# Attention order on ScalarE and TensorE, and the depthwise convolution's taps on GpSimd, in a hybrid decoder step with expert retrieval

## The chip, the cores and the metric

The kernel runs on one core of one Trainium2 chip. The metric is the device time of one execution in microseconds. The core's engines are TensorE (PE), VectorE (DVE), ScalarE (ACT), GpSimd (POOL) and SyncE (SP); each runs its own list of instructions in order, and they wait for each other by semaphores. Sixteen DMA engines move data between HBM and the on-chip memory (SBUF).

## The reference

One layer of a decoder trunk, on 1024 prompt tokens and on 64 sample tokens (8 sequences of 8), all in float32. Per token of width 1024:

```
z = x @ w_in                        # q, k, v (8 heads x 64), GLU value a and gate g (512 channels)
att  = causal attention over a mixture of three dilations, merged by softmax denominators
glu  = a * sigmoid(g)
conv[t, ch] = sum_{k=0..30} w[k, ch] * glu[t - 30 + k, ch] + b[ch]     # depthwise, causal
conv = silu(LayerNorm(conv))
x1   = LayerNorm(ALPHA * x + concat(att, conv) @ w_out)
y    = LayerNorm(ALPHA * x1 + PEER(x1))
```

PEER picks 128 of 16384 experts for each token (8 heads, two sets of 128 keys, the best 16 of each, the best 16 of their sums). An expert is a row u and a row v of 1024 numbers. Its part of the output is `gate * gelu(x1 . u) * v`.

## The kernel before

**Tiles and stages.** The tokens are cut into 8 prompt tiles of 128 tokens (`PT = 8`) and one tile of 64 sample tokens. The program runs in stages n = -1 to 9. Stage n does two things side by side: the expert sums of tile n, and the *front* of tile m = n + 1, that is attention, convolution, output projection, the first LayerNorm and the routing that picks the experts. Each stage has 128 places q = 4 g + i, with g = 0 to 31 and i = 0 to 3, and every engine's list is written out by the same loops over g and i. So the order of the work on each engine is fixed by hand, by the place in which a function is called.

**Expert sums of tile n.** For slot s (place q = s in stages 1 to 7) GpSimd issues a gather (L618): an indirect DMA that brings one expert row of 8 KB to each of the 128 partitions, 1 MB in all, into a ring of 9 rows (4 rows for tile 0). GpSimd waits for the ring row: the pair of slots that used it must have been summed by TensorE (semaphore `pv`; for tile 0 `v_done` of VectorE). Up to here its list holds nothing but the 1088 gathers. VectorE takes the dot product of x1 with u (`dot`, L1053, place s). For each two slots ScalarE applies Gelu (L770, in the same place), VectorE multiplies by the gate and spreads the weights on a diagonal (`weigh`, L1061 and L1064, one place later), and TensorE adds the two rows v, weighted, in PSUM (`values_pair`, L1399 and L1403, one place later). Tile 0 sums on VectorE instead (`first_values`, L1079).

**The front of tile m.** Attention has one head per group g, as a pipeline over four engines. Before the change, head h passes through these places:

- TensorE `scores` (L1270) in group h, i = 3: q times k into PSUM bank 2 and 3. It waits for the maximum of head h-1 (`sm_done`) and for the scaled copy of head h-2 (`att_done`).
- VectorE `weights_max` (L952, L955) in group h+1, i = 2: adds the bias and takes the maximum.
- ScalarE `weights_exp` (L685) in group h+1, i = 2: Exp with the sum.
- TensorE `weights_T` (L1281) and ScalarE `weights_T` (L694) in group h+1, i = 3: transposes and their copy to `pT`.
- TensorE `values` (L1292) in group h+2, i = 1: weights times v, into PSUM bank 2. As the scores of head h+1 lie in the same bank, it waits for their maximum, which VectorE takes in group h+2, i = 2.
- VectorE `weights_sum` (L962) in group h+2, i = 1, and ScalarE `normalise` (L702) in group h+2, i = 1: the copy of the result to `att`, scaled by one over the sum. It waits for the values matmuls (`pv_done`).

ScalarE loads a table when it goes from Gelu to Exp and back.

**Convolution.** The GLU output of all tokens is in HBM (`glu_scratch`). For tile m SyncE issues the load of its 158 columns into `gl` (L524) once the routing of tile m-1 is done (`a_route`). VectorE then runs 31 taps, `taps(m, k)`, spread over the places q = 1 to 39 by `tap_at`. Each tap is four instructions of 128x128, one for each 128 channels (L917 for k = 0, L920 for the rest). In group 10, i = 1, TensorE transposes the sums (`conv_rows`, L1309) when the semaphore `cv` shows them complete, and LayerNorm, Silu and the output projection follow. Tile 0's taps (L941, L944) and those of the sample tile (L929, L932) have their own lines.

**The rest of a stage.** In places 6 to 11 VectorE ends the tile before (`residual`, `ln2_end`). From place 69 to 127 VectorE runs the routing of tile m (L998 to L1030), one head in 7 places.

Of the kernel before, what the change touches and what calls it, by code (L numbers as in the profile page):

```python
# [10 lines left out]
ALU = mybir.AluOpType  # L11
# [3 lines left out]
P = 128  # L15
# [6 lines left out]
PT = SEQ // P  # L22
TILES = PT + 1
# [3 lines left out]
CT = CC // P  # L27
CK = 31
# [8 lines left out]
PH = 8  # L37
# [138 lines left out]
def tap_at(q):  # L176
    return range(q * CK // TAP_SPAN, (q + 1) * CK // TAP_SPAN) if q < TAP_SPAN else range(0)
# [31 lines left out]
def build(nc, I, O):  # L209
# [5 lines left out]
    with ctx:  # L215
# [3 lines left out]
        def at(off, shape, dt=F32):  # L219
            names[0] += 1  # L220
            return nc.alloc_sbuf_tensor_at(f"t{names[0]}", shape, dt, offset=base + off)

        def sem(name):
            return ctx.enter_context(nc.semaphore(name))
# [14 lines left out]
        qT = at(o_s, [P, CT, P])  # L239
        conv = at(o_s + 2048, [P, CT, P])  # L240
        cn = at(o_s + 4096, [P, CC])
        sm = at(o_s + 6144, [P, 2, SEQ])
        pT = at(o_s + 16384, [P, SEQ])
        att = at(o_s + 20480, [P, AW])
# [100 lines left out]
        pads = sem("pads")  # L345
        glu_done = sem("glu_done")
        cv = sem("cv")
        cvs = sem("cvs")
        q_out = [sem(f"q_out{i}") for i in range(2)]
        glu_out = [sem(f"glu_out{i}") for i in range(3)]  # L350
# [84 lines left out]
        def slots(t):  # L435
            return SLOTS if t < PT else SLOTS // 2
# [159 lines left out]
        @block.gpsimd  # L596
        def _(pool):
            def gather(t, s):
                if s % TOP == 0 and t < PT:
                    pool.wait_ge(a_route, PH * t + s // TOP + 1)  # L600
                elif s == 0:
                    pool.wait_ge(id_up, 16)
                r, use = spot(t, s)
                if t == 0:
                    if s >= FIRST_RING:
                        pool.wait_ge(v_done, s - FIRST_RING + 1)
                else:
                    k = (t - 1) * SLOTS + s
                    if k >= RING:
                        pool.wait_ge(pv, (k - RING) // 2 + 1)  # L610
                    elif k < FIRST_RING:
                        pool.wait_ge(v_done, SLOTS - FIRST_RING + k + 1)
                    elif k == FIRST_RING:
                        pool.wait_ge(proj_done, len(UNITS))
                        pool.wait_ge(glu_done, 3 * CT)
                        for i in range(2):
                            pool.wait_ge(q_out[i], 64)
                pool.indirect_dma_start(ring[:, r, :], None, I["expert_uv"],  # L618
                                        bass.IndirectOffsetOnAxis(ap=idn[t % 2][:, s:s + 1], axis=0)).then_inc(landed[r], 16)

            for t in range(TILES):
                for s in range(slots(t)):
                    gather(t, s)

        @block.scalar
        def _(act):
# [201 lines left out]
                                x1_rows(PT)  # L828

            def front(m, g, i):  # L830
                if i == 1 and 2 <= g < PH + 2:
                    normalise(m, g - 2)
                if i == 2 and 1 <= g <= PH:
                    weights_exp(m, g - 1)
                if i == 3 and 1 <= g <= PH:
                    weights_T(m, g - 1)
                for h in range(PH):
                    if g == QUERY_AT[h] and i == 3:
                        query_copy(m, h)
                        if h == 0:  # L840
                            x1_rows(m)
                if i != 2:
                    return
                if g == 11:
                    conv_std(m)
                if g == 12:
                    conv_swish(m)
                    attended(m)
                    route_loads(m)
                if g == 14:  # L850
                    ln1_std(m)
                if g == 15:
                    x1_transposed(m)
                for h in range(PH):
                    if g == QUERY_AT[h] + 1:
                        score_copy(m, h)
# [31 lines left out]
        def _(dve):  # L888
# [19 lines left out]
                    dve.wait_ge(state_in, 16)  # L908
                    dve.tensor_copy(gluS[:, i, :, PAST:], glu_st[:, i % 3, tn:tn + sn].rearrange("p (b t) -> p b t", b=NB)).then_inc(glus_kept, 1)

            def taps(m, k):
                if k == 0:
                    dve.wait_ge(gl_in, 16 * m)
                for i in range(CT):
                    w, src, dst = cwT[:, i, k:k + 1], gl[:, i, k:k + P], conv[:, i, :]
                    if k == 0:
                        dve.tensor_scalar(dst, src, w, cwT[:, i, CK:CK + 1], ALU.mult, ALU.add).then_inc(cv, 1)  # L917
                    else:
                        dve.wait_ge(cv, TAPS * m + CT * (k - 1) + i + 1)
                        dve.scalar_tensor_tensor(dst, src, w, dst, ALU.mult, ALU.add).then_inc(cv, 1)  # L920

            def sample_taps(k):
                if k == 0:
                    dve.wait_ge(glus_kept, CT)
# [10 lines left out]
            for i in range(CT):  # L935
                gated(0, i)
                dve.wait_ge(glu_done, i + 1)
                for k in range(CK):
                    w, src, dst = cwT[:, i, k:k + 1], gl[:, i, k:k + P], conv[:, i, :]
                    if k == 0:  # L940
                        dve.tensor_scalar(dst, src, w, cwT[:, i, CK:CK + 1], ALU.mult, ALU.add).then_inc(cv, 1)  # L941
                    else:
                        dve.wait_ge(cv, CK * i + k)
                        dve.scalar_tensor_tensor(dst, src, w, dst, ALU.mult, ALU.add).then_inc(cv, 1)  # L944

            def weights_max(m, h):
                u = PH * m + h
# [217 lines left out]
                    gates_end(PT, gate_events(PT), range(PH))  # L1165

            def front(m, g, i):
                for k in tap_at(4 * g + i) if m else ():
                    taps(m, k)
                if i == 1 and 2 <= g < PH + 2:  # L1170
                    weights_sum(m, g - 2)
                if i == 2 and 1 <= g < PH + 1:
                    weights_max(m, g - 1)
                if g == 11 and i == 0:
                    conv_var(m)
                if g == 11 and i == 3:
                    conv_norm(m)
                if g == 14 and i in (0, 1):
                    ln1_half(m, i)
                if g == 15 and i == 0:  # L1180
                    ln1_end(m)
                h, at_ = divmod(4 * g + i - ROUTE_AT, ROUTE_STEP)
                if 0 <= h < PH:
                    if at_ in (0, 2):
                        route_side(m, h, at_ // 2)
                    if at_ == 4:
                        route_pairs(m, h)
                    if at_ == 5:
                        route_experts(m, h)
                if m == 0 and at_ == ROUTE_STEP - 1 and 0 <= h < EARLY_GATES:  # L1190
                    gates(0, range(h, h + 1))
                if m == 0 and at_ == 1 and 1 <= h <= EARLY_GATES:
                    gates_end(0, h, range(h - 1, h))
                if g == 31 and i == 1:
                    gates(m, range(0 if m else EARLY_GATES, PH))
                if g == 31 and i == 3:
                    gates_end(m, gate_events(m), range(0 if m else EARLY_GATES, PH))
# [35 lines left out]
        def _(pe):  # L1233
# [66 lines left out]

            def conv_rows(m):
                if m < PT:
                    pe.wait_ge(cv, TAPS * (m + 1))
                    pe.wait_ge(sm_done, PH * (m + 1))
                else:
                    pe.wait_ge(cvs, TAPS)
                src = conv if m < PT else convS
                for c in range(CT):
                    last = pe.transpose(bank[3][0:rows(m), c * P:(c + 1) * P], src[:, c, :], ident[:, :])  # L1309
                last.then_inc(c_tr, 1)  # L1310
# [171 lines left out]
                                x1_rows(PT)  # L1482

            def front(m, g, i):
                if i == 1 and 2 <= g < PH + 2:
                    values(m, g - 2)
                if i == 3 and 1 <= g < PH + 1:
                    weights_T(m, g - 1)
                if i == 3 and g < PH:
                    scores(m, g)  # L1490
                for h in range(PH):
                    if g == QUERY_AT[h] and i == 3:
                        queries(m, h)
                        if h == 0:
                            x1_rows(m)
                    if g == QUERY_AT[h] + 1 and i == 1:
                        key_scores(m, h)
                if g == 13 and i in (1, 3):
                    out_projection(m, i // 2)
                if i != 1:  # L1500
                    return
                if g == 10:
                    att_transposes(m)
                    conv_rows(m)
                if g == 12:
                    conv_back(m)
                if g == 15:
                    x1_transposes(m)
# [68 lines left out]
```

## Time and profile before

| | us |
|---|---|
| median of 3 runs | 3743.29 |
| lowest, highest | 3739.91, 3750.01 |
| the profiled execution | 3747.08 |
| its span, first to last instruction | 3745.3 |

| engine | busy us | share of the span |
|---|---|---|
| VectorE | 2799.2 | 75% |
| TensorE, matmuls | 2592.0 | 69% |
| GpSimd | 1236.1 | 33% |
| ScalarE | 681.2 | 18% |

How to read it: the durations come from one profiled execution, whose own time is the 3747.08 us, and its instructions fill 3745.3 us of it. The queue of the gathers moved 1140.92 MB and its packets took 76.1% of the time of the 16 DMA engines; all queues together moved 1385.68 MB, a mean of 370 GB/s. The mean granted TensorE clock was 0.826 of full speed.
### The profile page before, as it was taken

The numbers are of one execution on the slowest core, as the hardware profiler recorded it, in microseconds if no ns is written. First come the engines' busy times: TensorE is split into PE (matmuls) and PEld (weight loads), VectorE is DVE, ScalarE is ACT, GpSimd is POOL, SyncE is SP. The second block draws the span as 40 slices with busy tenths as digits, with TensorE's granted clock in tenths as the row PEclk, the third lists the DMA queues.
The fourth block names the chain that finished last, engine by engine and source line by source line (L and its number), as shares of the span: only waits on it lengthen the run. The fifth ranks groups of instructions, "written<-read, shape, count | busy, mean of one in ns | idle before, by whom it ended". The sixth has DMA issues, their size and how long they took to land.

```text
span 3745.3 us, 39494 instructions
## 1 busy us (share of the span) xinstructions
PE 2592.0 (69%) x13744; PEld 1193.5 (32%) x13744; DVE 2799.2 (75%) x7472; ACT 681.2 (18%) x1478; POOL 1236.1 (33%) x1092
## 2 busy tenths in 40 slices
PE   7864347736775777677677766776787666779766
PEld 5433124532232223233323332333233322234311
DVE  5177867898789868986897689768976894356965
ACT  1210122002200321032013200320132002121000
POOL 0022212123443444434443434344434432233242
PEclk8987668867887888888788888887888878889889
DMA  9977898979999999999999999999989999999698
GB/s 341 343 296 258 303 371 311 400 278 355 398 417 381 361 381 421 395 367 375 415 391 347 381 421 390 344 369 421 393 336 368 420 409 422 418 420 396 261 384 342
DMA packets 217512, 1385.68 MB, mean 370 GB/s; under 512 B 27417, under 2 KB 38169, under 8 KB 66649
## 3 DMA queue, kind: packets, MB, share of 16 engines
q0 software_dynamic: 156672, 1140.92, 76.1%
q1 hardware_dynamic: 40384, 142.88, 10.4%
q10 hardware_dynamic: 20256, 99.35, 6.7%
q8 instruction: 109, 1.79, 0.2%
q14 instruction: 91, 0.74, 0.1%
HBM read 1369.94 MB, written 80.04 MB: 387 GB/s over the span
## 4 chain that ended last, share of the span: by engine, by line
DVE 30%; PE 26%; DMA 25%; issue 13%; ACT 3%; POOL 2%; ACTq 0%; SPq 0%; DVEq 0%; POOLq 0%
DMA t<-in_expert_uv,t 25%; PE psum L1403 12%; DVE t L1053 8%; PE psum L1250 3%; PE psum L1292 3%; DVE psum L1079 2%; PE psum L1328 2%; POOL t L618 2%; PE psum L1360 2%; DVE t L1064 2%; DVE t L1001 2%; DVE t L999 2%; PE psum L1270 2%; DVE t L1002 2%; DVE t L1000 1%
## 5 line engine op out<-in xcount | busy, mean ns | idle before, releaser
L618 POOL DMA_INDIRECT t<-in_expert_uv,t x1088 | 1235.9, 1136 | 2479.9 <-PE psum L1399 982.0
L1403 PE MATMUL psum<-t,t 64*64 64x512 f32 x4576 | 1323.4, 717 | 652.0 <-DVE t L1064 651.4
L1053 DVE CUSTOM_DVE_ANT_0 t<-t,t 128x1024 f32<-128x1024 f32 x1088 | 1322.2, 1222 | 529.6 <-DMA t<-in_expert_uv,t 520.0
L1399 PE MATMUL psum<-t,t 64*64 64x512 f32 x2592 | 807.9, 753 | 0.0
L1403 PEld LDWEIGHTS psum<-t,t 64*64 64x64 f32 x4576 | 329.0, 154 | 1422.6 <-DVE t L1064 798.4
L770 ACT ACTIVATE t<-t 128x2 f32<-128x2 f32 x544 | 110.6, 203 | 2038.0 <-DVE t L1053 2037.0
L1360 PEld LDWEIGHTS psum<-t,t 128*128 128x128 f32 x2304 | 286.3, 206 | 72.2 <-issue 63.4
L1360 PE MATMUL psum<-t,t 128*128 128x128 f32 (+1 forms) x2304 | 296.6, 291 | 4.8 <-ACT t L740 4.8
L1250 PE MATMUL psum<-t,t 128*128 128x128 f32 (+2 forms) x768 | 269.7, 512 | 6.6 <-DMA t<-in_xT 6.1
L920 DVE SCALAR_TENSOR_TENSOR t<-t,t,t 128x128 f32<-128x128 f32 x840 | 238.0, 346 | 0.0
L1292 PE MATMUL psum<-t,t 128*128 128x64 f32 x576 | 105.9, 348 | 162.7 <-issue 162.2
L1399 PEld LDWEIGHTS psum<-t,t 64*64 64x64 f32 x2592 | 182.3, 157 | 0.0
L1250 PEld LDWEIGHTS psum<-t,t 128*128 128x128 f32 x768 | 137.7, 210 | 123.3 <-issue 116.6
L1061 DVE TENSOR_TENSOR t<-t,t 128x2 f32<-128x2 f32 x480 | 75.9, 158 | 128.4 <-ACT t L770 126.3
L1079 DVE SCALAR_TENSOR_TENSOR psum<-t,t,psum 128x1024 f32<-128x1024 f32 x127 | 163.8, 1290 | 4.9 <-DVE t L1071 0.5
L1292 PEld LDWEIGHTS psum<-t,t 128*128 128x128 f32 x576 | 97.3, 256 | 211.1 <-issue 209.9
L1064 DVE TENSOR_TENSOR t<-t,t 128x128 f32<-128x128 f32 x480 | 140.2, 292 | 16.6
L1396 PE MATMUL psum<-t,t 128*64 128x512 f32 x256 | 118.9, 611 | 44.7 <-DVE t L1064 44.7
L1328 PE MATMUL psum<-t,t 128*128 128x512 f32 (+1 forms) x288 | 131.9, 614 | 3.6 <-ACT t L706 3.6
L770 ACT ACT_TABLE_LOAD x103 | 132.1, 1283 | 1.8
L1374 PE MATMUL psum<-t,t 128*128 128x128 f32 (+1 forms) x288 | 53.9, 316 | 112.4 <-ACT t L751 111.9
L1270 PE MATMUL psum<-t,t 64*128 64x512 f32 (+3 forms) x192 | 88.3, 571 | 39.7 <-DMA t<-q_scratch 39.2
(136 smaller groups left out, 2122.2 us busy)
## 6 DMA issues: line engine op xcount, KB each, us to landing
t<-in_wq_t ACTq DMA_DIRECT2D x63, 1024.0 KB, 9.6
out<-in_cache_k_win SPq DMA_DIRECT2D x8, 4080.0 KB, 46.2
out<-in_cache_v_win SPq DMA_DIRECT2D x8, 4080.0 KB, 40.9
t<-in_w_in_t ACTq DMA_DIRECT2D x44, 512.0 KB, 7.5
t<-in_kc_t SPq DMA_DIRECT2D x8, 2560.0 KB, 18.6
t<-in_vc_t SPq DMA_DIRECT2D x8, 2560.0 KB, 14.0
t<-in_expert_uv,t POOLq DMA_INDIRECT x1088, 11.0
t<-in_w_v_t ACTq DMA_DIRECT2D x6, 1024.0 KB, 10.0
```

The costliest lines, as they stand in the source:

```text
L618: pool.indirect_dma_start(ring[:, r, :], None, I["expert_uv"], bass.IndirectOffsetOnAxis(ap=idn[t % 2][:, s:s + 1], axis=0)).then_inc(land ...
L770: act.activation(d_, d_, ACT.Gelu).then_inc(a_gelu, 1)
L920: dve.scalar_tensor_tensor(dst, src, w, dst, ALU.mult, ALU.add).then_inc(cv, 1)
L1053: dve.tensor_tensor_reduce(out=ring[:, r, 0:D], in0=x1[t % 2][:, :], in1=ring[:, r, 0:D], scale=1.0, scalar=0.0, op0=ALU.mult, op1=ALU.add ...
L1064: dve.tensor_tensor(zt[:, k % Z_RING, :, :], ident2[:, :].unsqueeze(1).broadcast_to([P, 2, NS]), d2.unsqueeze(2).broadcast_to([P, 2, NS]), ...
L1079: dve.scalar_tensor_tensor(first_sum, ring[:, r, D:ROW], w_, first_sum, ALU.mult, ALU.add).then_inc(v_done, 1)
L1250: last = pe.matmul(dst[:, 0:tn + sn], w_ring[:, r, k, :], xT[p][:, k, 0:tn + sn], start=(k == 0), stop=(k == KD - 1))
L1292: last = pe.matmul(bank[2][:, 0:E], pT[:, j * P:(j + 1) * P], v[:, j, h * E:(h + 1) * E], start=(j == 0), stop=(j == m))
L1328: last = pe.matmul(bank[3 - half][0:rows(m), :], mixedT[:, k, 0:rows(m)], w_out[:, k, half * 512:(half + 1) * 512], start=(k == 0), stop=( ...
L1360: last = pe.matmul(bank[2 + h % 2][:, side * r:(side + 1) * r], w_[:, k, side * KEYC:(side + 1) * KEYC], x1T[:, k, 0:r], start=(k == 0), s ...
L1399: last = pe.matmul(AUX[t][half][NS - NS * a:P - NS * a, :], zt[NS * a:NS * a + NS, k % Z_RING, j, :], vv[NS * a:NS * a + NS, :], start=(c ...
L1403: last = pe.matmul(MAIN[t][half][NS * a:NS * a + NS, :], zt[NS * a:NS * a + NS, k % Z_RING, j, :], vv[NS * a:NS * a + NS, :], start=(c == ...
```

## The change

Three things change.

1. On ScalarE `normalise` of head g-2 moves from i = 1 of group g, ahead of `weights_exp` (i = 2), to i = 3 of the same group, behind `weights_exp` and the Gelu of that place and ahead of the copy of the transposed weights.
2. On TensorE `values` of head g-2 moves from i = 1 to i = 3 of group g, ahead of `weights_T` and `scores`.
3. The taps of tiles 1 to 7 leave VectorE. They run on GpSimd, in its list of gathers, in the same places (behind the gathers of the place). A tap is now a product of 128x512 with the weight spread along the tokens, into a new buffer `tap` (which lies where `cn` lies), and an addition of 128x512 to `conv`; each of the two waits for the one before. The first tap is the product straight into `conv` and the addition of the bias. The first tap of a tile waits for the load of `gl` and for the transposes of the tile before that read `conv`. The semaphore `cv` now counts GpSimd's instructions; tile 0's taps, which stay on VectorE, count on a new one, `cv0`.

```diff
@@ gpsimd
-            for t in range(TILES):
-                for s in range(slots(t)):
-                    gather(t, s)
+            def taps(m, k):
+                if k == 0:
+                    pool.wait_ge(gl_in, 16 * m)
+                    pool.wait_ge(c_tr, m)
+                n = 2 * CK * (m - 1) + 2 * k
+                w = cwT[:, :, k:k + 1].broadcast_to([P, CT, P])
+                if k == 0:
+                    pool.tensor_tensor(conv[:, :, :], gl[:, :, k:k + P], w, ALU.mult).then_inc(cv, 1)
+                    pool.wait_ge(cv, n + 1)
+                    w = cwT[:, :, CK:CK + 1].broadcast_to([P, CT, P])
+                    pool.tensor_tensor(conv[:, :, :], conv[:, :, :], w, ALU.add).then_inc(cv, 1)
+                else:
+                    pool.tensor_tensor(tap[:, :, :], gl[:, :, k:k + P], w, ALU.mult).then_inc(cv, 1)
+                    pool.wait_ge(cv, n + 1)
+                    pool.tensor_tensor(conv[:, :, :], conv[:, :, :], tap[:, :, :], ALU.add).then_inc(cv, 1)
+                pool.wait_ge(cv, n + 2)
+
+            for n in range(-1, TILES):
+                for q in range(SLOTS):
+                    for s in slots_at(n, q):
+                        gather(max(n, 0), s)
+                    for k in tap_at(q) if 1 <= n + 1 < PT else ():
+                        taps(n + 1, k)
@@ scalar, front(m, g, i)
-                if i == 1 and 2 <= g < PH + 2:
-                    normalise(m, g - 2)
                 if i == 2 and 1 <= g <= PH:
                     weights_exp(m, g - 1)
+                if i == 3 and 2 <= g < PH + 2:
+                    normalise(m, g - 2)
                 if i == 3 and 1 <= g <= PH:
                     weights_T(m, g - 1)
@@ vector, front(m, g, i)
-                for k in tap_at(4 * g + i) if m else ():
-                    taps(m, k)
@@ tensor, conv_rows(m) and front(m, g, i)
-                    pe.wait_ge(cv, TAPS * (m + 1))
+                    if m:
+                        pe.wait_ge(cv, 2 * CK * m)
+                    else:
+                        pe.wait_ge(cv0, TAPS)
...
-                if i == 1 and 2 <= g < PH + 2:
+                if i == 3 and 2 <= g < PH + 2:
                     values(m, g - 2)
```

## Rows read from the trace of the kernel before

**Rows 1.** The page, part 1: busy us, share of the span, instructions.
```profile
PE 2592.0 (69%) x13744; PEld 1193.5 (32%) x13744; DVE 2799.2 (75%) x7472; ACT 681.2 (18%) x1478; POOL 1236.1 (33%) x1092
```

**Rows 2.** Windows: places 0 to 40 of tiles 0 to 6, each engine's busy us.
```profile
core 0: us, PE busy (x) PEld busy (x) DVE busy (x) ACT busy (x) POOL busy (x), PEclk, DMA share, GB/s
434.90:574.90 140.00, 62.44 (x146) 32.08 (x144) 98.15 (x241) 37.80 (x67) 25.13 (x24) 0.62 0.93 349
847.90:974.20 126.30, 83.12 (x392) 29.78 (x392) 108.73 (x328) 37.74 (x70) 50.95 (x44) 0.77 0.90 356
1221.20:1346.00 124.80, 94.65 (x458) 35.51 (x454) 99.47 (x286) 40.06 (x72) 52.57 (x43) 0.85 0.89 348
1586.00:1712.90 126.90, 98.86 (x494) 41.84 (x490) 100.88 (x287) 41.71 (x72) 45.50 (x42) 0.84 0.89 348
1955.40:2089.40 134.00, 106.29 (x522) 47.28 (x518) 101.81 (x286) 43.57 (x72) 48.21 (x43) 0.83 0.87 329
2329.50:2465.40 135.90, 106.57 (x544) 47.42 (x540) 102.85 (x288) 44.94 (x72) 47.37 (x43) 0.86 0.86 325
2705.50:2844.00 138.50, 111.65 (x566) 50.20 (x562) 103.86 (x286) 46.75 (x72) 47.28 (x43) 0.86 0.84 322
```

**Rows 3.** Windows of tile 1: places 40 to 69, then 69 to 128.
```profile
974.20:1046.50 72.30, 56.57 (x328) 22.27 (x332) 51.53 (x130) 17.60 (x39) 33.22 (x29) 0.88 1.01 422
1046.50:1221.20 174.70, 111.84 (x708) 49.69 (x702) 165.28 (x508) 14.27 (x48) 65.48 (x56) 0.78 0.99 396
```

**Rows 4.** One attention head of tile 6: timeline (start, us, engine, line), then its window.
```profile
2783.24 1.97 PE L1292 MATMUL psum<-t,t 128*128 128x64 f32 x16 [2.86 <-issue]
2785.30 0.31 ACT L702 ACTIVATE t<-psum,t 128x64 f32<-128x64 f32 x1 [5.73 <-PE psum L1292]
2788.19 1.28 ACT L770 ACT_TABLE_LOAD   x1
2789.72 0.16 DVE L1061 TENSOR_TENSOR t<-t,t 128x2 f32<-128x2 f32 x1 [3.06 <-ACT t L770]
...
2783.24:2796.30 13.06, 10.29 (x60) 4.82 (x61) 9.89 (x29) 5.55 (x8) 4.45 (x5) 0.85 0.88 333
```

**Rows 5.** The page, part 5: the tap instructions, busy us and mean ns.
```profile
L920 DVE SCALAR_TENSOR_TENSOR t<-t,t,t 128x128 f32<-128x128 f32 x840 | 238.0, 346 | 0.0
```

**Rows 6.** Groups by line: elementwise instructions of VectorE, busy us and mean ns.
```profile
L1026 DVE TENSOR_TENSOR t<-t,t 128x512 f32<-128x512 f32 (+1 forms) x72 | 49.7, 691 | 2.5
...
L1108 DVE TENSOR_TENSOR t<-t,t 128x1024 f32<-128x1024 f32 (+1 forms) x9 | 11.0, 1224 | 0.3
```

**Rows 7.** Timeline: a dot, the gather that began under it, and the next.
```profile
2793.44 1.21 DVE L1053 CUSTOM_DVE_ANT_0 t<-t,t 128x1024 f32<-128x1024 f32 x1
2793.84 1.62 POOL L618 DMA_INDIRECT t<-in_expert_uv,t  x1 [2.82 <-PE psum L1399]
2795.77 0.94 POOL L618 DMA_INDIRECT t<-in_expert_uv,t  x1 [0.30 <-issue]
```

**Rows 8.** The line of the gathers: duration in ns, and landing.
```profile
L618 POOL DMA_INDIRECT t<-in_expert_uv,t x1088: 932/939/2182, 191.7 to 3715.3; - x182
...
DMA to landing us min/median/max: 5.4/11.0/38.3
```

**Rows 9.** Timeline and line: glu loads of tiles 1 and 6, landing, tile 6's start.
```profile
834.12 0.84 SPq L524 DMA_DIRECT2D t<-glu_scratch  x1
2699.56 0.63 SPq L524 DMA_DIRECT2D t<-glu_scratch  x1
...
DMA to landing us min/median/max: 5.3/8.7/9.3
...
2697.16 0.94 POOL L618 DMA_INDIRECT t<-in_expert_uv,t  x1 [0.30 <-issue]
2708.75 1.12 DVE L917 TENSOR_SCALAR t<-t,t 128x128 f32<-128x128 f32 x4 [0.47 <-DMA t<-glu_scratch]
```

More of the change, by code:

```diff
@@ L241, in build @@
         cn = at(o_s + 4096, [P, CC])
+        tap = at(o_s + 4096, [P, CT, P])
         sm = at(o_s + 6144, [P, 2, SEQ])
@@ L347, in build @@
         cv = sem("cv")
+        cv0 = sem("cv0")
         cvs = sem("cvs")
@@ L909, in gated @@
                     dve.tensor_copy(gluS[:, i, :, PAST:], glu_st[:, i % 3, tn:tn + sn].rearrange("p (b t) -> p b t", b=NB)).then_inc(glus_kept, 1)
[L911 to L920, printed above, removed]
             def sample_taps(k):
@@ L940, in _ @@
                     if k == 0:
-                        dve.tensor_scalar(dst, src, w, cwT[:, i, CK:CK + 1], ALU.mult, ALU.add).then_inc(cv, 1)
+                        dve.tensor_scalar(dst, src, w, cwT[:, i, CK:CK + 1], ALU.mult, ALU.add).then_inc(cv0, 1)
                     else:
-                        dve.wait_ge(cv, CK * i + k)
-                        dve.scalar_tensor_tensor(dst, src, w, dst, ALU.mult, ALU.add).then_inc(cv, 1)
+                        dve.wait_ge(cv0, CK * i + k)
+                        dve.scalar_tensor_tensor(dst, src, w, dst, ALU.mult, ALU.add).then_inc(cv0, 1)
             def weights_max(m, h):
```

## The prediction

> **What bounds the kernel now.** I read the page first: VectorE is busy 75% of the span, TensorE 69%, GpSimd 33% [rows 1]. No engine is full, so the bound changes from stage to stage and the page cannot say what one stage is worth. The second view cuts the span at the dot products, one for each of the 128 places of a tile. Tiles 1 to 6 (while the front of tiles 2 to 7 runs) take 365 to 376 us from first dot to first dot, in three parts. Places 0 to 40 take 124.8 to 138.5 us, 3.3 us a place, mean 131.1; VectorE is busy 75 to 86% of it, TensorE 66% (tile 1) to 81% (tile 6), the DMA engines 84 to 90% [rows 2]. Places 40 to 69 take 72.3 us, 2.5 a place, at 422 GB/s and a DMA share of 1.01: bound by the gathers' bytes. Places 69 to 128 have VectorE at 165.28 of 174.70 us, in the routing [rows 3]. Only the first part holds taps and attention. The third view is one head of attention in it, 13.06 us long for tile 6 (from the values matmuls of one head at 2783.24 to the next): TensorE had waited 2.86 us before those matmuls, since they need VectorE's maximum of the next head; ScalarE waited 5.73 us for them before its scaled copy, then came Exp, a table load and Gelu, and VectorE stood 3.06 us until that Gelu [rows 4]. So the part is a loop of VectorE, TensorE and ScalarE. GpSimd is busy only 46 to 53 us there [rows 2] and otherwise waits for free ring rows.
>
> **Taps off VectorE.** 840 instructions of 346 ns go, 120 per tile [rows 5], with 4 of L917: 34 us busy of the 102 in an average part, about 0.85 us a place. VectorE's own need falls to some 68 us in 131; it can't bound the part afterwards.
>
> **The scaled copy and the values matmuls two places later.** Exp no longer stands behind a copy that waits for matmuls that wait for VectorE. Per head that can remove up to the 3.06 us on VectorE and the 2.86 us on TensorE [rows 4]; they lie beside each other, so about 3 us a head, 8 heads, at most 25 us a tile, if nothing else is late. In place of it TensorE runs values, transposes and scores back to back, and the scores of a head now wait in the same place for a copy queued behind a Gelu; the table load before Gelu is 1.28 us [rows 4], beside the matmuls. I cost that at nothing: after it the VectorE maximum is three places away. What is late next is the question, and I say GpSimd.
>
> **Taps on GpSimd, its serial need.** From place 1 to 39 it has 31 taps of two instructions, 62 of 128x512, each waiting for the one before. The trace holds no arithmetic of that size on GpSimd. Lower end: VectorE's multiply of 128x512, 0.69 us; upper end: twice VectorE's 128x1024, 2.45 us. I take 1.22, the 128x1024 one once [rows 6], that is half of VectorE's rate, because it lies nearest to the one instruction of size that GpSimd has, the gather with 0.94 to 2.18 us [rows 8]. For the wait between two I take 0.1 us, ends 0 and the 0.30 between two gathers [rows 7]. So 62 x 1.32 = 81.8 us. A gather is 0.94 us and 0.30 to the next [rows 7, 8]: 1.24.
> The Trainium skill (GPSIMD Engine Reference, "Performance versus the Vector engine") gives 4497 ns for a two-input f32 operation of 2048 elements, twice VectorE's. A quarter is an estimate of 1.12 us; by it the 62 would cost 75.6 us instead of 81.8, 6 us less a tile. No row here shows it.
>
> **What the two engines take from each other.** A dot (1.21 us) started at 2793.44 and ended at 2794.65; a gather that began under it at 2793.84 took 1.62 us and ended 0.81 us after the dot, while the next, beside other VectorE work, took 0.94 [rows 7]. Gathers run from 0.93 to 2.18 us [rows 8]. So a dot already holds up GpSimd. The taps read SBUF all the time, 82 us of a part, and there are 40 dots of 1.22 us, 49 us, besides the weighings (0.16 + 0.29 us per pair). Bounds of GpSimd's loss: 0, and each dot with half a weighing in full, 1.22 + 0.23 = 1.45 us, 55 us for 38. I take 0.6 a dot, 23 us: GpSimd is in a tap about half of the time, a dot that arrives then waits for its end and costs the next tap about a dot; the other half costs a gather a few tenths. VectorE loses about as much and has the 34 us to pay it with.
> The Trainium skill (SBUF — State Buffer, "Who interferes with whom") says that a VectorE instruction with two SBUF inputs contends with a GpSimd instruction that reads SBUF, and the second fully blocks. The row agrees for a gather under a dot; what it does to an elementwise instruction no run here shows. With that rule in full the loss is nearer the 55 us, without it 0.
>
> **The new wait.** The first tap waits for the load of glu rows. That load is issued (L524) 13.8 us before the first dot of tile 1 and about 6 us before it in tiles 2 to 6, and lands a median 8.7 us later; VectorE stood 0.47 us for it in tile 6 [rows 9]. But GpSimd is ahead of VectorE by the ring: in tile 6 the gather of slot 2 was issued at 2697.16, the load landed at about 2708.3 [rows 9]. It and those after it now stand behind the wait, and behind them the dots. A gather lands a median of 11.0 us after its issue [rows 8], so VectorE stands for them early in the tile.
>
> **The sum per tile.** From the landing of glu to the dot of place 40, GpSimd needs 38 gathers, 47.1, plus 81.8, plus 23: 152 us; then 11 us until slot 40 has landed: 163. Now the same stretch is, in order of tiles 1 to 6 (part's end from [rows 2], issue plus 8.7 from [rows 9]; the issues of tiles 2 to 5, which aren't shown, are 6.7, 6.0, 5.9 and 5.9 us ahead of their first dot): 131, 123, 124, 131, 133 and 136, mean 129.7. The difference is 33 us, six times 199. The places after 40 give nothing back: they run at the DMA limit or at VectorE's. Tile 0 has only 25 gathers in its first 40 places and takes 140 us for them [rows 2]: GpSimd needs 31 + 82 + 10 = 123; VectorE's 34 us come free but its four-row ring makes each gather's latency count, and a gather now stands behind taps. I put it at 0, ends -20 and +20. The tail and the sample tile have no part in it.
> The profiled execution took 3747.1 us (span 3745.3); 3747.1 + 199 = 3946. The median of the runs is 3743.3, 3.8 lower: **3942 us**, 5.3% slower.
>
> **Rivals.**
> - GpSimd keeps up: faster. The two stretches are equal when 47.1 + 62x + lock = 118.7, so with 23 us lost to the dots a tap instruction with its wait must cost under 0.78 us, without any loss under 1.15. Then the part falls to the next bound: bytes at 422 GB/s, 126.3 x 356 / 422 = 107 us, and TensorE's 112 us in tile 6, in sum some 130 less over six tiles; the wait at the tile's start keeps about 40 of it, tile 0 gives 20: 3747 - 110, median 3633. For it: the loop of rows 4 does lose 3 us a head. Against: it needs GpSimd nearly at VectorE's rate. 20%.
> - GpSimd is serial, but the two don't block each other: 47.1 + 81.8 - 118.7 = 10 us, 62 in all: 3805. Against it stands the gather stretched by a dot. 12%.
> - Everything cancels within 0.3%: a tap instruction at the balance point. 3%.
> - A tap instruction costs 2 us or more, from the stride of the input or from changing between gathers and arithmetic: 47.1 + 62 x 2.1 + 30 = 207, 89 a tile, 532: 4275. 8%.
> The likeliest, GpSimd bound with blocking, has 57%, with its own range 3850 to 4050 (lost to the dots 12 to 35 us, a tap instruction with its wait 1.25 to 1.42: 18 to 51 us a tile).
>
> **Range and chances.** Uncertainty of the costs and the edge of the faster case: 3670 to 4090. It leaves out the dear instruction (8) and some 12 of the faster case. A measurement of this kernel tells 0.3%, 11 us, from no change. Faster 0.20, same 0.04, slower 0.76. The bounds taken all together (0.69 without loss, 2.45 with all) reach further, but no row favours either end.
>
> **What would show it.** Right: in places 0 to 40 GpSimd's busy share goes from 37% to over 80%, with almost no wait for TensorE between its gathers; VectorE's wait for landings there grows from a few us to tens, its busy time falls by less than 34 us because dots become longer than 1.22 us; DMA share falls below 0.8; places 40 to 128 are unchanged; the idle of L1061 behind ScalarE shrinks. The tap instruction's mean should be 1.1 to 1.6 us with the blocking. Wrong: GpSimd still waiting for TensorE in the part, a tap instruction under 0.8 us, dots of constant length, or a changed time after place 40.

## The result, and the profile after

The changed kernel takes 3944.2 us (median of 4 runs), the kernel before 3746.7 us beside it: ratio 1.0526, 95% interval 1.0503 to 1.0550. The forecast was 3942 us, 5.3% slower. (One of the four runs, at a granted TensorE clock of 0.544 in place of 0.82, took 4352.8 us; the interval is made without it.) The profiled execution spans 3939.4 us, 194.1 more than before.

The page after, parts 1, 2 and 5. The columns are as in [rows 1, 5]; L620 is now the gather, L1064 the dot, L635 the product and L637 the addition of a tap, L1072 and L1075 the weighing, L1415 the sums on TensorE.

```profile
span 3939.4 us, 39267 instructions
PE 2626.3 (67%) x13744; PEld 1184.7 (30%) x13744; DVE 2801.5 (71%) x6604; ACT 682.1 (17%) x1478; POOL 1880.8 (48%) x1526
POOL 0022562149634964396438744874478433223232
...
L620 POOL DMA_INDIRECT t<-in_expert_uv,t x1088 | 1265.1, 1163 | 1949.8 <-PE psum L1411 714.2
L1064 DVE CUSTOM_DVE_ANT_0 t<-t,t 128x1024 f32<-128x1024 f32 x1088 | 1451.6, 1340 | 873.9 <-DMA t<-in_expert_uv,t 864.0
...
L637 POOL TENSOR_TENSOR t<-t,t 128x512 f32<-128x512 f32 x210 | 365.3, 1739 | 16.5
...
L635 POOL TENSOR_TENSOR t<-t,t 128x512 f32<-128x512 f32 x210 | 231.4, 1102 | 4.8
...
L1072 DVE TENSOR_TENSOR t<-t,t 128x2 f32<-128x2 f32 x480 | 147.4, 307 | 13.0 <-ACT t L792 10.9
```

VectorE lost 868 instructions and is busy as long as before (2801.5 against 2799.2 us, [rows 1]). Its wait for gathers went from 520 to 864 us. GpSimd's line in 40 slices has a peak of 6 to 9 tenths at the start of each tile, where it had 4; in the chain of work that ended last, part 4 of the page, GpSimd has 19% of the span where it had 2%.

The windows of places 0 to 40 of tiles 1 to 6 answer to [rows 2]; columns as there. Then those of places 40 to 69 and 69 to 128 of tile 6.

```profile
856.40:1012.80 156.40, 87.50 (x392) 29.12 (x392) 124.53 (x203) 37.57 (x70) 137.95 (x102) 0.72 0.77 271
1264.80:1422.70 157.90, 103.52 (x458) 35.94 (x454) 97.43 (x164) 40.23 (x72) 140.23 (x105) 0.77 0.76 268
1667.90:1826.20 158.30, 106.35 (x496) 41.41 (x492) 99.44 (x162) 41.99 (x72) 142.04 (x104) 0.78 0.76 268
2071.60:2229.10 157.50, 104.41 (x520) 42.03 (x516) 103.18 (x162) 43.50 (x72) 141.87 (x104) 0.83 0.76 269
2474.90:2632.90 158.00, 111.98 (x542) 46.60 (x538) 101.36 (x163) 45.06 (x71) 141.97 (x105) 0.82 0.76 269
2877.70:3033.10 155.40, 113.09 (x559) 47.95 (x555) 102.48 (x163) 46.56 (x71) 140.10 (x104) 0.82 0.77 273
```
```profile
3033.10:3111.50 78.40, 59.36 (x337) 24.45 (x340) 46.63 (x101) 17.89 (x40) 36.57 (x31) 0.87 1.01 420
3111.50:3277.60 166.10, 111.48 (x708) 51.12 (x702) 154.30 (x452) 14.26 (x48) 64.16 (x56) 0.80 1.01 416
```

What to see: GpSimd is busy a mean of 140.7 of 157.3 us, 89%, and the part takes 155 to 158 us in every tile, while before it grew from 125 to 138.5 us with the attention's length. That fits an engine whose work does not depend on the tile. The DMA share was 0.84 to 0.90 and is 0.77 now. The 194 us by stretch: the six first parts +157 (943.5 against 786.4), places 40 to 69 +29 (78.4 against a mean of 73.7 in each tile), places 69 to 128 0, everything up to the first dot of tile 1 +8.5, tiles 7 and 8 together +0.4.

The timeline of tile 6 shows how the two engines hold each other up (start, us, engine, line; lines of VectorE and GpSimd).

```profile
2963.66 2.50 DVE L1064 CUSTOM_DVE_ANT_0 t<-t,t 128x1024 f32<-128x1024 f32 x1 [3.08 <-DMA t<-in_expert_uv,t]
2964.01 1.05 POOL L635 TENSOR_TENSOR t<-t,t 128x512 f32<-128x512 f32 x1
2965.14 2.13 POOL L637 TENSOR_TENSOR t<-t,t 128x512 f32<-128x512 f32 x1
2966.09 0.08 DVE L1064 DVE_READ_ACCUMULATOR2_ANT t<- 128x1 f32 x1
2966.09 1.20 DVE L1072 TENSOR_TENSOR t<-t,t 128x2 f32<-128x2 f32 x1
2967.32 0.29 DVE L1075 TENSOR_TENSOR t<-t,t 128x128 f32<-128x128 f32 x1
2967.53 1.22 DVE L963 CUSTOM_DVE_ANT_0 t<-psum,t 128x1024 f32<-128x1024 f32 x1
```

The dot, 1.22 us when nothing is in its way, takes 2.50: it ends 1.10 us after the product, so nearly all of its work was done behind it. It had begun 0.35 us before the product, beside a gather, and lost its turn all the same. That is no single case: 41 products began up to 0.64 us after a dot did, and each of these dots ended 1.09 us after the product; only a product that began 0.70 us or more after the dot waited for it. The addition then stands behind the dot: 2.13 us. The weighing of two numbers per partition, 0.16 us, takes 1.20 because it stands behind the addition and ends with it. L963, which reads one operand from PSUM, keeps its 1.22 in such places: 40 of its 64 runs overlap a tap instruction, and none takes longer than 1.23. The durations of the lines (ns min/median/max):

```profile
L635 POOL TENSOR_TENSOR t<-t,t x210: 1042/1055/1908, 431.7 to 3024.0; 128x512 f32<-128x512 f32 x105
L637 POOL TENSOR_TENSOR t<-t,t x210: 1259/2123/2351, 432.8 to 3025.1; 128x512 f32<-128x512 f32 x105
L1064 DVE CUSTOM_DVE_ANT_0 t<-t,t x1088: 1204/1225/2781, 194.0 to 3923.3; 128x1024 f32<-128x1024 f32 x182
```

The addition has two humps: 98 of 210 take 1.26 to 1.40 us, 112 take 2.12 to 2.35, and in 109 of these 112 a dot was under way when the addition began, in none of the 98. Before, no dot was longer than 1.30 us; now 153 of 1088 are.

### The profile page after: what moved, and what is told of

Its sections match the earlier page's. It is cut to its first block, busy times and chain, and to the rows that moved or that the text cites. A ratio compares the mean times of both kernels' runs of the same rounds, so it can differ in the third digit from the quotient of the medians.

```text
span 3939.4 us, 39267 instructions
## 1 busy us (share of the span) xinstructions
PE 2626.3 (67%) x13744; PEld 1184.7 (30%) x13744; DVE 2801.5 (71%) x6604; ACT 682.1 (17%) x1478; POOL 1880.8 (48%) x1526
## 4 chain that ended last, share of the span: by engine, by line
DVE 28%; DMA 26%; POOL 19%; PE 15%; issue 11%; ACT 1%; SPq 0%; POOLq 0%; ACTq 0%; DVEq 0%
DMA t<-in_expert_uv,t 25%; DVE t L1064 8%; POOL t L620 8%; POOL t L637 7%; PE psum L1415 6%; POOL t L635 4%; DVE psum L1090 2%; PE psum L1340 2%; PE psum L1259 2%; DVE t L1012 2%; DVE t L1010 2%; DVE t L1013 2%; DVE t L1075 1%; DVE t L1011 1%; DVE t L1009 1%
## 5 line engine op out<-in xcount | busy, mean ns | idle before, releaser
L620 POOL DMA_INDIRECT t<-in_expert_uv,t x1088 | 1265.1, 1163 | 1949.8 <-PE psum L1411 714.2
L1064 DVE CUSTOM_DVE_ANT_0 t<-t,t 128x1024 f32<-128x1024 f32 x1088 | 1451.6, 1340 | 873.9 <-DMA t<-in_expert_uv,t 864.0
L1415 PE MATMUL psum<-t,t 64*64 64x512 f32 x4576 | 1375.5, 742 | 908.3 <-DVE t L1075 903.2
L1415 PEld LDWEIGHTS psum<-t,t 64*64 64x64 f32 x4576 | 338.8, 158 | 1748.5 <-DVE t L1075 1097.5
L1411 PE MATMUL psum<-t,t 64*64 64x512 f32 x2592 | 844.2, 783 | 0.0
L637 POOL TENSOR_TENSOR t<-t,t 128x512 f32<-128x512 f32 x210 | 365.3, 1739 | 16.5
L1372 PEld LDWEIGHTS psum<-t,t 128*128 128x128 f32 x2304 | 284.0, 204 | 71.3 <-issue 60.8
L635 POOL TENSOR_TENSOR t<-t,t 128x512 f32<-128x512 f32 x210 | 231.4, 1102 | 4.8
L1411 PEld LDWEIGHTS psum<-t,t 64*64 64x64 f32 x2592 | 187.9, 162 | 0.2
L1259 PEld LDWEIGHTS psum<-t,t 128*128 128x128 f32 x768 | 136.6, 209 | 120.5 <-issue 113.8
L1072 DVE TENSOR_TENSOR t<-t,t 128x2 f32<-128x2 f32 x480 | 147.4, 307 | 13.0 <-ACT t L792 10.9
L1075 DVE TENSOR_TENSOR t<-t,t 128x128 f32<-128x128 f32 x480 | 140.2, 292 | 16.6
L1301 PE MATMUL psum<-t,t 128*128 128x64 f32 x576 | 93.7, 318 | 61.0 <-issue 60.5
L1301 PEld LDWEIGHTS psum<-t,t 128*128 128x128 f32 x576 | 85.1, 228 | 130.8 <-issue 129.0
```

Of the source, the lines that this page charges most:

```text
L635: pool.tensor_tensor(tap[:, :, :], gl[:, :, k:k + P], w, ALU.mult).then_inc(cv, 1)
L637: pool.tensor_tensor(conv[:, :, :], conv[:, :, :], tap[:, :, :], ALU.add).then_inc(cv, 1)
L1064: dve.tensor_tensor_reduce(out=ring[:, r, 0:D], in0=x1[t % 2][:, :], in1=ring[:, r, 0:D], scale=1.0, scalar=0.0, op0=ALU.mult, op1=ALU.add ...
L1075: dve.tensor_tensor(zt[:, k % Z_RING, :, :], ident2[:, :].unsqueeze(1).broadcast_to([P, 2, NS]), d2.unsqueeze(2).broadcast_to([P, 2, NS]), ...
L1259: last = pe.matmul(dst[:, 0:tn + sn], w_ring[:, r, k, :], xT[p][:, k, 0:tn + sn], start=(k == 0), stop=(k == KD - 1))
L1372: last = pe.matmul(bank[2 + h % 2][:, side * r:(side + 1) * r], w_[:, k, side * KEYC:(side + 1) * KEYC], x1T[:, k, 0:r], start=(k == 0), s ...
```

## The experiments

All times are medians beside runs of the kernel before on the same chip (3743 to 3747 us); the ratio is to those.

**The parts of the change apart.** e1 is the kernel before with ScalarE's `normalise` and TensorE's `values` at i = 3:

```diff
-                if i == 1 and 2 <= g < PH + 2:
-                    normalise(m, g - 2)
                 if i == 2 and 1 <= g <= PH:
                     weights_exp(m, g - 1)
+                if i == 3 and 2 <= g < PH + 2:
+                    normalise(m, g - 2)
...
-                if i == 1 and 2 <= g < PH + 2:
+                if i == 3 and 2 <= g < PH + 2:
                     values(m, g - 2)
```

> Only parts 1 and 2 of the change (scaled copy and values matmuls two places later); the taps stay on VectorE. Theory (the attention part was a loop of VectorE, TensorE and ScalarE that stood about 3 us a head): faster than before, each first part of tiles 1 to 6 shorter by 8 to 20 us, near 3650 us (3600 to 3700), the idle of VectorE behind Gelu nearly gone, VectorE over 85% busy in that part. Rival (the copy's wait was cover for something else, GpSimd or the bytes): 3735 to 3750 us. Rival (scores now wait for the copy behind Gelu): over 3760 us.

3629.7 us, ratio 0.9689 (0.9673 to 0.9705): **117 us faster than before**, and faster than both kernels of this case. Its windows of places 0 to 40, tiles 1 and 6; then VectorE's wait for Gelu (L770) in the kernel before (us in total, times, longest), and who waited for Gelu in e1:

```profile
839.60:953.40 113.80, 79.82 (x390) 27.42 (x391) 108.24 (x328) 37.37 (x69) 51.98 (x43) 0.77 0.96 388
2613.10:2722.60 109.50, 95.89 (x556) 42.03 (x552) 103.60 (x286) 45.91 (x71) 52.72 (x42) 0.96 0.97 392
```
```profile
DVE t L1061 <- ACT t L770: 126.3, 73, 5.8
...
who waited for it (us, times):
  DVE t L1061: 14.9, 47
```

The wait of VectorE for Gelu fell from 126 us in 73 waits to 14.9. The six parts sum to 653 us against 786, that is 22 us a tile in the mean. I had expected 8 to 20 in each: tiles 1 to 3 are 13 to 21 us shorter, tiles 4 to 6 27 to 29. The DMA share is 0.96 to 0.99, at 387 to 400 GB/s where places 40 to 69 reach 421, so the part runs near the limit of the gathers' bytes. Places 40 to 69 take 2.9 us a tile more than before and give 17 us back.

e2 is the other half: the changed kernel with the order of before.

```diff
+                if i == 1 and 2 <= g < PH + 2:
+                    normalise(m, g - 2)
...
-                if i == 3 and 2 <= g < PH + 2:
-                    normalise(m, g - 2)
...
-                if i == 3 and 2 <= g < PH + 2:
+                if i == 1 and 2 <= g < PH + 2:
                     values(m, g - 2)
```

> Only part 3 (taps on GpSimd); the order of attention as before. Theory (GpSimd sets the pace of places 0 to 40, the order is hidden beneath it): within 0.5% of the changed kernel, 3925 to 3965 us. Rival (the two add up, the order gave its 3 us a head in the changed kernel too): 4000 to 4080 us.

3954.0 us, ratio 1.0554 (1.0536 to 1.0572). With the order it was 3944.2: the same order that is worth 117 us alone is worth about 10 beside the taps, and the two intervals (1.0536 to 1.0572 and 1.0503 to 1.0550) overlap, so it may be worth nothing. Moving the taps costs 207 us on the old order and 314 on the new.

e7 moves ScalarE's copy alone, TensorE's `values` stays at i = 1.

> The kernel before with ScalarE's scaled copy alone two places later; TensorE's values matmuls stay at i = 1, the taps on VectorE. Theory (Exp and Gelu stood behind the copy, and VectorE behind Gelu): it has most of the gain of e1_order_only, 3640 to 3680. Rival (TensorE's own wait for VectorE's maximum carries the gain): 3710 to 3745.

3635.1 us, ratio 0.9704 (0.9685 to 0.9722), 5 us under the range that I had expected and not told apart from e1. VectorE's wait for Gelu is 13.9 us here. The gain is ScalarE's order; TensorE's own move adds nothing that can be measured.

**Size of GpSimd's instructions.** e3 leaves the count of instructions and waits of the changed kernel and cuts each to the first of the four channel groups, which leaves out three quarters of the convolution of tiles 1 to 7.

```diff
+                w = cwT[:, 0:1, k:k + 1].broadcast_to([P, 1, P])
...
-                    pool.tensor_tensor(tap[:, :, :], gl[:, :, k:k + P], w, ALU.mult).then_inc(cv, 1)
+                    pool.tensor_tensor(tap[:, 0:1, :], gl[:, 0:1, k:k + P], w, ALU.mult).then_inc(cv, 1)
...
```

> The changed kernel, but each tap instruction on GpSimd covers 128x128 in place of 128x512: three quarters of the convolution of tiles 1 to 7 are left out. Same number of instructions, waits and semaphores. Theory (GpSimd's serial time and the blocking by the length of its instructions): a tap instruction takes 0.3 to 0.45 us, GpSimd needs some 75 us of the part, so the part falls to the next bound and the whole to 3600 to 3680 us, faster than before. Rival (the count of waits and the wait for the glu load at the start of the tile set the loss): stays over 3800 us.

3674.2 us, ratio 0.9804 (0.9787 to 0.9820). The instructions take 0.40 to 1.50 us, and are as uneven as the wide ones:

```profile
L638 POOL TENSOR_TENSOR t<-t,t x210: 452/457/1502, 435.7 to 2755.0; 128x128 f32<-128x128 f32 x105
```

An addition takes 0.45 us when free, and up to 1.05 us more otherwise. The mean of product and addition is 0.69 us, not the 0.3 to 0.45 that I had expected; the kernel's time fell in the expected range even so. 270 us of the changed kernel's time hang on the length of its 434 tap instructions, not on their number.

**Serial time and blocking apart.** e4 puts a memset of the same size in the place of each tap instruction, e5 two memsets, which occupies GpSimd for nearly as long as an unblocked tap instruction does, without a read. Both leave out the convolution of tiles 1 to 7.

```diff
-                    pool.tensor_tensor(tap[:, :, :], gl[:, :, k:k + P], w, ALU.mult).then_inc(cv, 1)
-                    pool.wait_ge(cv, n + 1)
-                    pool.tensor_tensor(conv[:, :, :], conv[:, :, :], tap[:, :, :], ALU.add).then_inc(cv, 1)
+                pool.memset(tap[:, :, :], 0.0)
+                pool.memset(conv[:, :, :], 0.0).then_inc(cv, 1)
+                pool.wait_ge(cv, n + 1)
+                pool.memset(tap[:, :, :], 0.0)
+                pool.memset(conv[:, :, :], 0.0).then_inc(cv, 1)
```

These are e5's lines. e4 has `tap`'s memset alone in front of the wait and `conv`'s alone behind it.

> The changed kernel, but each of the 62 tap instructions of a tile is a memset of 128x512 on GpSimd, which writes and reads nothing: the convolution of tiles 1 to 7 is left out. Theory (a VectorE instruction with two SBUF inputs and a GpSimd instruction that reads SBUF block each other): dots keep 1.22 us throughout, none over 1.35, and no two-humped duration of the memsets. Rival (GpSimd's writes block as well): dots stretched beyond 1.35 us as in the changed kernel. The time follows the memset's duration, which no trace shows: at 0.5 us about 3650, at 1.1 us about 3850.

> As e4_write_only, but each tap instruction is two memsets of 128x512, so that GpSimd is occupied about as long as by the real tap instructions when nothing blocks them (1.06 and 1.26 us), and still reads nothing; the convolution of tiles 1 to 7 is left out. It splits the loss into GpSimd's serial time and the blocking. Theory (both count): GpSimd needs 38 x 1.24 + 62 x 1.17 = 120 us, the first part of a tile 120 to 130 us, the whole 3720 to 3790 us, so that some 150 to 220 us of the changed kernel are the blocking. Rival (serial time alone): 3900 to 3950. Rival (blocking alone, serial time hidden): at e4's 3640.

e4: 3639.5 us in one run. e5: 3749.3 us (median of 10), ratio 1.0015 (1.0002 to 1.0028). First the memset and the dot of e4, then the dot of e5, then e5's window of tile 6.

```profile
L631 POOL MEMSET t<- x217: 524/524/1017, 430.5 to 2720.6; 128x512 f32 x109
...
L1058 DVE CUSTOM_DVE_ANT_0 t<-t,t x1088: 1204/1225/1300, 196.2 to 3621.5; 128x1024 f32<-128x1024 f32 x182
```
```profile
L1060 DVE CUSTOM_DVE_ANT_0 t<-t,t x1088: 1205/1225/1299, 195.0 to 3724.7; 128x1024 f32<-128x1024 f32 x182
...
2704.90:2834.20 129.30, 108.14 (x561) 48.33 (x557) 74.12 (x163) 46.53 (x71) 109.48 (x168) 0.85 0.91 332
```

Of 434 memsets 175 began under a dot, and all but two took 0.52 to 0.55 us; no dot is longer than 1.30. GpSimd's memsets and a dot pass each other; its multiplications and additions, which read two operands from SBUF, and a dot do not. No run has arithmetic on GpSimd with a single SBUF operand, so which of the two it takes stays open. The first parts take 125 to 129 us with e5. So with the new order GpSimd's serial time costs 3749 - 3630 = 120 us over e1, and what comes on top with the real taps 3944 - 3749 = **195 us**. Two memsets are 1.07 us, a free tap instruction 1.16 in the mean; 62 x 0.09 x 6 = 33 us of the 195 may be that. The blocking is 160 to 195 us, 27 to 32 a tile. The 120 us is net of VectorE's relief; over e8 below, which has no taps but the first, the serial time costs 139 us.

**The wait at the tile's start.** e6 is the changed kernel with the span of the taps begun at place 4; as the first place of the span gets none, they lie in places 5 to 39, and four more gathers go out ahead of the first tap.

```diff
-    return range(q * CK // TAP_SPAN, (q + 1) * CK // TAP_SPAN) if q < TAP_SPAN else range(0)
+    s, w = q - 4, TAP_SPAN - 4
+    return range(s * CK // w, (s + 1) * CK // w) if 0 <= s < w else range(0)
```

> The changed kernel with the 31 taps of a tile in places 4 to 39 in place of 1 to 39, so that three more gathers go out before GpSimd waits for the glu load. Theory (the wait at the tile's start is idle time of the engine that sets the pace, 58 us in seven tiles): 20 to 50 us faster than the changed kernel, 3895 to 3925. Rival (the wait is paid back by the ring's lead, or the denser taps cost as much): within 10 us of it, 3934 to 3954.

3943.9 us, the changed kernel's time. My theory failed here. GpSimd's wait for the glu load did fall, from 57.8 us to 3.7; but its wait for TensorE (L1415 in the changed kernel, L1416 here) rose from 325.7 to 370.1, and the additions from a mean of 1739 to 1795 ns. At the start of tile 6 the changed kernel's GpSimd waits 8.58 us for the load, until 2877.65; e6's stands nearly as long at the same point for a ring row:

```profile
2877.65 1.05 POOL L630 TENSOR_TENSOR t<-t,t 128x512 f32<-128x512 f32 x1 [8.58 <-DMA t<-glu_scratch]
...
2883.27 1.45 POOL L621 DMA_INDIRECT t<-in_expert_uv,t  x1 [7.98 <-PE psum L1416]
```

So the gathers that now go ahead of the load gain nothing. That the same 31 taps are packed into 35 places in place of 39 is a second difference, which no run takes apart.

**What VectorE's relief is worth.** e8 (new order) and e9 (old order) keep the taps on VectorE and do the first of the 31 alone.

```diff
                 for k in tap_at(4 * g + i) if m else ():
-                    taps(m, k)
+                    if k == 0:
+                        taps(m, k)
...
-                    pe.wait_ge(cv, TAPS * (m + 1))
+                    pe.wait_ge(cv, TAPS + CT * m)
```

> As e1_order_only (new order, taps on VectorE), but only the first of the 31 taps of tiles 1 to 7 is done: the rest of their convolution is left out. It is what moving the taps could bring at best with the new order. Theory (with the new order the first part runs near the limit of the gathers' bytes, DMA share 0.96 to 0.99, and VectorE's taps lie beneath it): within 0.6% of e1_order_only, 3605 to 3635 us. Rival (VectorE is the next bound, 103 of 108 us busy): 3550 to 3600 us.

> The kernel before, old order of attention, with only the first of the 31 taps of tiles 1 to 7: what moving the taps could bring at best with the old order. Theory (the old order was a loop through VectorE, in which the taps of a head, 3.4 us busy, stood in series): 3630 to 3680 us, that is either cure alone reaches the same floor. Rival (the loop stood on TensorE and ScalarE, VectorE's taps lay in its idle time): 3700 to 3745 us.

e8: 3609.9 us, ratio 0.9637 (0.9610 to 0.9664). e9: 3637.4 us, ratio 0.9714 (0.9686 to 0.9742). Taking 30 of 31 taps off VectorE at no cost to any engine is worth 106 us with the old order and 20 with the new. The window of tile 6, e8 and then e9, and e9's wait of VectorE for Gelu:

```profile
2604.90:2712.60 107.70, 99.49 (x554) 44.84 (x550) 74.17 (x167) 46.39 (x71) 49.23 (x42) 0.91 0.97 394
```
```profile
2615.20:2728.50 113.30, 98.55 (x556) 43.57 (x552) 72.69 (x168) 46.10 (x70) 47.26 (x42) 0.94 0.95 373
...
DVE t L1061 <- ACT t L770: 132.4, 77, 6.3
```

In e8 VectorE's busy time is 74 us in place of 104, and the part is 2 us shorter than e1's. In e9 VectorE waits for Gelu as long as in the kernel before (132 against 126 us), and the kernel is 106 us faster all the same: my reading is that the old order lost time because the taps and that wait stood one behind the other on VectorE. Taking away either one brings the six first parts to 652.5 us (e1) or 654.0 (e9), at DMA shares of 0.95 to 0.99.

## Why the prediction was right, step by step

- **What bounds the kernel: right.** The first part was a loop with slack, and only it changed much. GpSimd went from 37% to 89% there, with no wait for TensorE in tile 6's part, the DMA share to 0.77, and VectorE waited 51 us for landings in tile 6's part where it had waited 2.3. The tap instruction's mean is 1.42 us, within the 1.1 to 1.6 forecast. (A slip in the working, without weight: tiles 1 to 6 took 365 to 378 us, not 365 to 376.)
- **Taps off VectorE: the instruction count right, the rest not as put.** I wrote that its busy time would fall by less than 34 us. In tile 6 it fell by 1.4 (103.86 to 102.48): the blocked dots and weighings took nearly all of it. In tile 1, where the sample tile's taps stay on VectorE and are blocked too (16.6 us in place of 7.75), it rose, from 108.73 to 124.53.
- **The order: size right, and hidden as forecast.** At most 25 us a tile, I said; e1 has 22 in the mean of the first parts, and 27 to 29 in tiles 4 to 6, above that bound. That only ScalarE's copy matters I had not said, nor that taking the taps off VectorE brings as much (e9). Beside the taps it gives about 10 us, if anything (e2).
- **GpSimd's need: the sum right, two terms off by 7 us against each other.** I had 152 us from the first tap to the gather of slot 40. The windows of tile 6 show it, for GpSimd as a whole, then L637, L635 and L620:

```profile
2877.65:3027.50 149.85, 135.52 (x100) 0.84 0.77 273
...
2877.65:3027.50 149.85, 51.37 (x30) 0.84 0.77 273
...
2877.65:3027.50 149.85, 33.13 (x30) 0.84 0.77 273
...
2877.65:3027.50 149.85, 48.07 (x38) 0.84 0.77 273
```

  Tiles 1 to 6 have 150 to 156 us, mean 152. Free of dots it would be 31 x (1.055 + 1.26) = 71.8, 38 x 0.94 = 35.7 and the gaps, 14.4: 122, where I had 128.9; a tap instruction with its wait was mis-sized at 1.32, by the same split it is (122 - 47.1) / 62 = 1.21. The rest, 30 us, is the blocking, where I had 23, mis-sized too: some 17 us of it are in the tap instructions and 12 in the gathers. A dot that waited for a product always landed on the addition behind it, and 112 of 210 additions took 0.87 us more. Of the 12 us in the gathers about 7 are not new: in e5, where the same stretch takes 119.7 us, the 38 gathers already take 42.6 in place of 35.7.
- **From the gather to its dot: mis-sized.** I took the 11.0 us of [rows 8]. With the DMA engines at 0.77 the gather of slot 40 was 5.5 to 5.8 us ahead of its dot (3027.5 and 3033.1 in tile 6). That is 5 us a tile less in the first part. Another 2 us a tile come from the start: the load of glu rows landed a median 6.0 us after its issue and not the 8.7 of [rows 9], so the first tap of a tile began a mean 0.4 us before its first dot, where the forecast's starting point lay 1.4 us behind it. Together they make +157 in the first parts and not +199.
- **The wait at the start: no price.** I counted from the landing of the load as if GpSimd could do nothing useful before. e6 shows that it couldn't in any case.
- **Tile 0 at 0, ends 20:** +8.5 up to the first dot of tile 1.
- **Places 40 to 128 unchanged: wrong by 29 us** for 40 to 69, right for the rest. Before, the gather of slot 40 went out 18 us ahead of its dot (2825.8 and 2844.0, tile 6), now 5.5: the ring's lead is spent, and the places after 40 pay for it. The rate there didn't fall, it is 420 to 422 GB/s (406 to 422 before); at that rate 78.4 us move 33.0 MB where 30.7 were moved, 2.3 MB or two gathers more that hadn't landed before place 40. e1, e4 and e8 have 76 to 79 us there too: their first parts are short and would leave more bytes to this one, which no run takes apart. The forecast itself had named a changed time after place 40 as a sign of being wrong.
- **Luck.** The forecast of +199 us lay wholly in the first parts. They brought 157, 42 less, and the two terms put at nothing brought 29 and 8.5. That these nearly cancel is luck, and so is the 0.1% between 3942 and 3944; the sign, the range and GpSimd as the engine that binds are not.
- **The rivals' prices:** "GpSimd keeps up" was given 3633 us; e4, with 0.53 us an instruction and no reads, has 3639. "Serial without blocking" was given 3805 and e5 has 3749; its two memsets and a wait are near 1.15 us, the threshold that I gave without blocking, and it stands 0.15% from the kernel before.

The Trainium skill's figure (GPSIMD Engine Reference, "Performance versus the Vector engine"), from which 1.12 us was estimated, is near what was measured: 1.055 us with a spread weight, 1.26 with two full operands. Its rule of two SBUF inputs (SBUF — State Buffer, "Who interferes with whom") agrees with what the rows here can tell: the dot blocks tap instructions and is blocked by them, L1072 is blocked, the memsets and L963 are not. That the second of the two is the one that waits, as the prediction has it, doesn't hold by the order of their starts: of the products that began under a dot, the 41 early ones went first.

## What to carry to other kernels

Before work moves from one engine to another, take it away altogether in one run: e9 says that the relief of VectorE was worth 106 us at best, e8 that after a change of two lines on ScalarE it was worth 20, and neither pays for what the taps cost on GpSimd: 3954 - 3637 = 317 us over e9, 3944 - 3610 = 334 over e8. Price elementwise work on GpSimd beside a VectorE that reads two SBUF operands at its serial time plus the dots it meets: here 120 us and up to 195. A stretch whose length no longer depends on the tile's size is a hint at the engine that binds it.

## What the runs showed of the hardware

- A gather that begins under a dot ends 0.81 us after it [rows 7]; so do 330 of the 335 gathers in the kernel before that began under a dot and took over 1.1 us. Seven that began in the dot's first 0.04 us took 0.93 to 0.94 and were not held. A plain TENSOR_TENSOR of VectorE with two SBUF operands holds a gather too, here L1026 of the kernel before:

```profile
1436.77 0.69 DVE L1026 TENSOR_TENSOR t<-t,t 128x512 f32<-128x512 f32 x1
1436.82 1.45 POOL L618 DMA_INDIRECT t<-in_expert_uv,t  x1 [0.30 <-issue]
```

  The gather ends 0.81 us after L1026, and all five gathers that began within 0.06 us of an L1026 took 1.45 us. The 63 that began under L1079, which has an operand in PSUM, took 0.93 to 0.95. A memset, which also writes SBUF from GpSimd, isn't held at all, so the gather's hold by a dot is something else than a memset's write.
- On GpSimd, a product whose second operand is one number per channel group spread over 128 columns takes 1.055 us, an addition of two full operands 1.26, at 128x512; at 128x128 the two take a median of 0.42 and 0.46.
- L1075, which has two SBUF operands too (292 ns, 480 times), was never longer than 333 ns. It doesn't speak against the blocking: it follows L1072, which takes the wait upon itself, and no tap instruction was under way when one of the 480 began.
